# Probability transposes of an attention kernel: whole tiles by head, or 64 queries on each half of the array

## The reference, cut to what matters

```python
h = x @ w_in                                   # one projection for all head groups
# group B: 8 query heads on 2 key/value heads, dense; group A: 8 heads, masked with log multiplicities
s = q @ k.T * scale
p = softmax(s)
o = p @ v
f = concat(out_a * silu(ga), out_b * silu(gb)) @ w_out
y = layer_norm(alpha * x + f)
```

## Time and profile before

| | |
|---|---|
| median of 3 runs | 478.27 us (476.8 to 478.57) |
| profiled execution | 480.86 us, of which the span of its trace 479.0 us |
| PE busy | 438.4 us, 92% of the span |
| DVE, POOL, ACT busy | 282.1, 240.6, 217.0 us |
| probability transposes | 320 instructions |

### The profile page before, as it was taken

One profiled execution on the slowest core, in us unless ns is written; L12 is line 12 of the kernel. 1 busy time (PEld: TensorE's weight loads), 2 busy tenths in 40 slices (PEclk: granted clock), 3 DMA queues, 4 the chain that ended last, 5 costly groups with the idle time before them and its releaser, 6 DMA issues.

```text
span 479.0 us, 8874 instructions
## 1 busy us (share of the span) xinstructions
PE 438.4 (92%) x3310; PEld 403.8 (84%) x3310; DVE 282.1 (59%) x782; ACT 217.0 (45%) x499; POOL 240.6 (50%) x330
## 2 busy tenths in 40 slices
PE   1999979799889999999999999999899879999990
PEld 1999969787789999998899999999678659999990
DVE  1543675438978667464666767654576775433664
ACT  3342213443446455565555546555465774121222
POOL 1227944775644555334334854734523871455664
PEclk9999989899989999999999999999899898999996
DMA  6612212010201102001010101102000290231122
GB/s 237 252 44 62 71 30 85 22 45 23 67 8 37 46 24 65 26 22 50 28 58 22 49 23 42 45 23 67 1 23 23 73 325 1 80 96 45 68 107 90
DMA packets 23290, 29.99 MB, mean 63 GB/s; under 512 B 1872, under 2 KB 19408, under 8 KB 23248
## 3 DMA queue, kind: packets, MB, share of 16 engines
q1 hardware_dynamic: 22816, 29.30, 19.2%
q10 hardware_dynamic: 432, 0.13, 0.1%
HBM read 26.28 MB, written 3.15 MB: 61 GB/s over the span
## 4 chain that ended last, share of the span: by engine, by line
PE 67%; POOL 11%; DVE 8%; issue 6%; DMA 4%; ACT 4%; SPq 1%; ACTq 0%; DVEq 0%; POOLq 0%
PE bank L545 15%; PE bank L547 14%; PE bank L546 14%; PE bank L506 10%; PE bank L635 7%; PE bank L597 6%; DMA raw<-w_out 3%; POOL scr L1113 2%; DMA h_a<-x_prompt 2%; POOL tanh L1099 2%; POOL w_lo L1084 1%; DVE tmp_s L852 1%; ACT prob L761 1%; DVE h_qb L892 1%; DVE prob L927 1%
## 5 line engine op out<-in xcount | busy, mean ns | idle before, releaser
L545 PE MATMUL bank<-w_hi,t_lo 128*128 128x256 f32 x576 | 168.3, 292 | 2.7 <-POOL t_lo L1158 2.0
L546 PE MATMUL bank<-w_lo,t_hi 128*128 128x256 f32 x576 | 164.8, 286 | 0.0
L547 PE MATMUL bank<-w_hi,t_hi 128*128 128x256 f32 x576 | 164.7, 286 | 0.0
L1152 POOL TENSOR_SCALAR prob<-prob,den 128x512 f32<-128x512 f32 (+1 forms) x96 | 61.3, 643 | 117.0 <-DVE den L948 117.0
L545 PEld LDWEIGHTS bank<-w_hi,t_lo 128*128 128x128 f32 x576 | 112.3, 195 | 4.0 <-issue 1.4
L547 PEld LDWEIGHTS bank<-w_hi,t_hi 128*128 128x128 f32 x576 | 112.3, 195 | 0.0
L546 PEld LDWEIGHTS bank<-w_lo,t_hi 128*128 128x128 f32 x576 | 112.2, 195 | 0.0
L1084 POOL TENSOR_TENSOR w_lo<-raw,w_hi 128x512 fp32r<-128x512 f32 x52 | 67.4, 1306 | 35.2 <-ACT w_hi L714 34.6
L770 ACT ACTIVATE p_hi<-bank 128x512 fp32r<-128x512 f32 x80 | 47.2, 591 | 51.2 <-PE bank L506 51.1
L761 ACT ACTIVATE prob<-prob,nmax 128x512 f32<-128x512 f32 (+1 forms) x96 | 61.8, 645 | 15.9 <-DVE nmax L927 15.9
L714 ACT ACTIVATE w_hi<-raw 128x512 fp32r<-128x512 f32 x62 | 38.4, 629 | 48.9 <-DMA raw<-w_in 23.3
(11 more groups left out here) (110 smaller groups left out, 753.6 us busy)
## 6 DMA issues: line engine op xcount, KB each, us to landing
raw<-w_in SPq DMA_DIRECT2D x50, 256.0 KB, 2.8
raw<-w_out SPq DMA_DIRECT2D x16, 256.0 KB, 3.0
h_a<-x_prompt SPq DMA_DIRECT2D x7, 512.0 KB, 6.9
h_a<-x_sample SPq DMA_DIRECT2D x4, 512.0 KB, 9.8
y_prompt<-h_a SPq DMA_DIRECT2D x8, 256.0 KB, 2.1
y_sample<-h_a SPq DMA_DIRECT2D x4, 256.0 KB, 2.1
cst<-consts SPq DMA_DIRECT2D x1, 960.0 KB, 9.7
h_a<-x_prompt SPq DMA_DIRECT2D x2, 256.0 KB, 3.6
```

The source lines that it names most:

```text
L545: nc.tensor.matmul(out, a_lo, b_hi, start=(m == 0), stop=False)
L546: nc.tensor.matmul(out, a_hi, b_lo, start=False, stop=False)
L547: ins = nc.tensor.matmul(out, a_hi, b_hi, start=False, stop=(m == KT - 1))
L1152: ins = nc.gpsimd.tensor_scalar(e, e, den[:, s, t:t + 1], 0.5, ALU.mult, ALU.mult)
```

## The change

The four 128x128 transposes of a head become eight of 64 rows by 128 keys: queries 0 to 63 on the upper row half of the array and queries 64 to 127 on the lower, with the matching 64x64 block of the identity as the moving operand. Upper halves of both heads go to bank 4, lower halves of both to bank 5. Instructions alternate between the halves, as those of `scores` do. `pt_ready` now comes for each half, when both heads are through; `prob_high` and `prob_low` work by half (both heads) where they worked by head; the layout of `p_hi` and `p_lo` follows, and `values` of either head waits for both halves.

```diff
-        p_hi = sb("p_hi", [P, 2, 2, SEQ], F32R)
-        p_lo = sb("p_lo", [P, 2, 2, SEQ], F32R)
+        p_hi = sb("p_hi", [P, 2, 2, 2, 4, P // 2], F32R)
+        p_lo = sb("p_lo", [P, 2, 2, 2, 4, P // 2], F32R)
...
-            def prob_transposes(v):
-                pe.wait_ge(scaled, v + 1)
-                if v >= 2:
-                    pe.wait_ge(pt_lo_done, v - 1)
-                transpose_batch(pt_ps[v % 2], [prob[:, v % PRING, n * P:(n + 1) * P] for n in range(4)]) \
-                    .then_inc(pt_ready, 1)
+            def prob_transposes(w):
+                if w:
+                    pe.wait_ge(pt_lo_done, 2 * w)
+                for s in range(2):
+                    v = 2 * w + s
+                    pe.wait_ge(scaled, v + 1)
+                    for n in range(4):
+                        for half in range(2):
+                            rows = slice(P // 2 * half, P // 2 * (half + 1))
+                            at = (4 * s + n) * P // 2
+                            ins = nc.tensor.transpose(pt_ps[half][:, at:at + P // 2],
+                                                      prob[rows, v % PRING, n * P:(n + 1) * P], ident[rows, rows])
+                            if s == 1 and n == 3:
+                                ins.then_inc(pt_ready, 1)
...
-                pe.wait_ge(pt_lo_done, 2 * w + s + 1)
+                pe.wait_ge(pt_lo_done, 2 * w + 2)
...
-                o = o_ps[s][:, 0:2 * P].rearrange("p (t q) -> p t q", t=2)
+                o = o_ps[s][:, 0:2 * P].rearrange("p (t h q) -> p t h q", t=2, h=2)
...
-                        hi, lo = (a[:, s, :, n * P:(n + 1) * P] for a in (p_hi, p_lo))
+                        hi, lo = (a[:, :, :, s, n, :] for a in (p_hi, p_lo))
...
-            def prob_high(v):
-                act.wait_ge(pt_ready, v + 1)
...
+            def prob_high(w, half):
+                act.wait_ge(pt_ready, 2 * w + half + 1)
...
-                    dve.wait_ge(pt_ready, v - PRING + 1)
+                    dve.wait_ge(pt_ready, 2 * ((v - PRING) // 2) + 2)
...
-            def prob_low(v):
-                dve.wait_ge(pt_hi_done, v + 1)
...
+            def prob_low(w, half):
+                dve.wait_ge(pt_hi_done, 2 * w + half + 1)
```

More of the change, by code:

```diff
@@ L623, in values @@
                 base, keys = (QT, ST) if sample else (0, QT)
-                o = o_ps[s][:, 0:2 * P].rearrange("p (t q) -> p t q", t=2)
+                o = o_ps[s][:, 0:2 * P].rearrange("p (t h q) -> p t h q", t=2, h=2)
                 for n in range(keys):
                     if sample:
-                        hi, lo = (a[:, s, 0, :].rearrange("p (t n q) -> p t n q", n=ST, q=P)[:, :, n, :]
+                        hi, lo = (a[:, 0, :, s].rearrange("p h (t n) q -> p t n h q", n=ST)[:, :, n]
                                   for a in (p_hi, p_lo))
                     else:
-                        hi, lo = (a[:, s, :, n * P:(n + 1) * P] for a in (p_hi, p_lo))
+                        hi, lo = (a[:, :, :, s, n, :] for a in (p_hi, p_lo))
                     v = values_of(kv)[:, base + n, :]
@@ L655, in _ @@
                 if LAG <= w < NW + LAG:
-                    for s in range(2):
-                        prob_transposes(2 * (w - LAG) + s)
+                    prob_transposes(w - LAG)
                 for b in steps[w]:
@@ L763, in exps @@
                 ins.then_inc(exp_done, 1)
-            def prob_high(v):
-                act.wait_ge(pt_ready, v + 1)
[L767 to L770, removed]
+            def prob_high(w, half):
+                act.wait_ge(pt_ready, 2 * w + half + 1)
+                k = w % UNITS
+                if k % 2 == 0 and w:
+                    act.wait_ge(pv_done, group_of(2 * w - 1) + 1)
+                nc.scalar.activation(p_hi[:, k % 2, half].rearrange("p s n q -> p (s n q)"), pt_ps[half][:],
+                                     ACT.Copy).then_inc(pt_hi_done, 1)
             def copy_low(G):
@@ L809, in _ @@
                     if LAG <= w < NW + LAG:
-                        prob_high(2 * (w - LAG) + s)
+                        prob_high(w - LAG, s)
                     if w < NW:
@@ L930, in mask_max @@
                 ins.then_inc(s_masked, 1)
-            def prob_low(v):
-                dve.wait_ge(pt_hi_done, v + 1)
-                p, k, s = unit(v)
-                nc.vector.tensor_tensor(p_lo[:, s, k % 2, :], pt_ps[s][:], p_hi[:, s, k % 2, :].bitcast(F32),
-                                        ALU.subtract).then_inc(pt_lo_done, 1)
+            def prob_low(w, half):
+                dve.wait_ge(pt_hi_done, 2 * w + half + 1)
+                hi, lo = (a[:, w % UNITS % 2, half].rearrange("p s n q -> p (s n q)") for a in (p_hi, p_lo))
+                nc.vector.tensor_tensor(lo, pt_ps[half][:], hi.bitcast(F32), ALU.subtract).then_inc(pt_lo_done, 1)
             def t_low(b):
@@ L1018, in _ @@
                     if LAG <= w < NW + LAG:
-                        prob_low(2 * (w - LAG) + s)
+                        prob_low(w - LAG, s)
                     if w < NW:
```

## The result

The changed kernel takes 476.76 us (median of 20 runs, 472.14 to 480.86) beside 478.82 us of the kernel before on the same chips (20 runs): ratio 0.9944, interval 0.992 to 0.9968. It is 2.1 us faster, where 8.7 was forecast. The profiled execution took 477.14 us, its span 475.3.

A forecast was written before the change was run, and what follows sets the result against it. PE was taken to bound steps 5 to 29, chains through DVE, ACT and POOL its waits elsewhere. Gains of 10.3 us less 0.15 and 1.5 give 8.7: 478.27 - 8.7 = 469.6 us, range 465.5 to 478.

The forecast's parts named there:

- the clock: Rival: one 3.4 us half-clock stretch after PE stalls, more or less, moves time up to 1.7 us; no chance given.
- The pair, 0.06: Two half transposes, one on each row half, run side by side and take 0.06 us together.
- The stretch: Last scores to PE's next work: 0.915 us before a projection instead of 1.26, 0.805 in sample steps instead of 1.14.
- the drain and the late load: After the last half transposes: 0.10 us draining for the array-mode change, then an unhidden load, 0.11 for a projection.
- The rival of the pairs: Transpose pairs take 0.12 us, not 0.06, so the kernel gets slower, 482 us; chance 0.13.
- the one in between: Rival: transpose pairs take near 0.09 us, losing 5.9 us in 28 steps, total 476 us; chance 0.12.
- Steps 5 to 29, 9.2 - 0.15 = 9.05 us: Shorter transposes gain 9.2 us where PE is always busy; waits of values in steps 9, 14, 24 lose 0.15.
- third rival, the chains: Softmax chain or copies hold PE back, losing some 0.3 us in about 10 steps, total 473 us; chance 0.15.
- Steps 31, 32 and 35, 1.1 us: Projection work follows these transposes with no wait in the way, so 1.1 us more is gained.
- Step 37, 1.5 us: Late second head delays ACT's first copy and the values: 1.3 us lost, 2.8 with half clock, taken as 1.5.

The follow-up runs named there:

- e11: The changed kernel run once more without any edit, in another set: 474.65 us, ratio 0.9916 to the kernel before.
- e3: The changed kernel plus 60 thrown-away matmuls where PE has to wait for other engines: 469.43 us, ratio 0.9803 to the kernel before.
- e4: The kernel before plus the 60 thrown-away matmuls where PE has to wait: 477.05 us, ratio 0.9949 to the kernel before.
- e8: The changed kernel with half transposes in steps 5 to 29 alone, by head elsewhere: 471.95 us, ratio 0.987 to the kernel before.
- e9: The changed kernel with by-head transposes in steps 5 to 29, halves elsewhere: 481.04 us, ratio 1.0044 to the kernel before.
- e1: The changed kernel with by-head transposes in steps 4, 34, 37 and 39: 472.01 us, ratio 0.9843 to the kernel before.
- e7: The changed kernel issuing each head's four upper half transposes, then its four lower ones: 473.31 us, ratio 0.9914 to the kernel before.
- e6: The changed kernel with by-head transposes in step 37 alone: 475.66 us, ratio 0.991 to the kernel before.
- e2: The kernel before with the change's two later waits but its old full-height transposes: 483.75 us, ratio 1.0096 to the kernel before.

## Why the prediction was wrong, point by point

The step that failed is the rival of **the clock**: one stretch of 3.4 us more or less, up to 1.7 us either way, inside the range. In the median run it is 17 us more, and 5.5 to 6.6 us are lost by it; 19 of the 20 runs of the change have more time at 1.2 GHz than any of the 65 of the kernel before. I took the clock as noise around the forecast; it is a result of the change. That it is the clock is shown from three sides: the same program at 0.967 in place of 0.952 has a span 4 us shorter (e11), with thrown-away matmuls in both kernels the difference is 7.6 us in place of 2.1 (e3 against e4), and it is lost in the steps where PE stands and in no other (e8 against e9; in steps 5 to 29 the granted clock is 1.00 in every window shown). Ahead of each of the four falls shown PE had stood. The prediction said of these steps that gains on PE there turn into longer waits, and priced the waits at nothing. The price is that PE's work behind the wait runs at 1.2 GHz.

**The pair, 0.06** (bounds 0.055 and 0.12): 0.062, which is one matmul each 0.031. **The stretch** of 0.915 behind a projection and 0.805 in a sample step: 0.92 in step 16, and 0.71 recorded and 0.11 of a load that was not hidden, 0.82, in the sample step 29. The sum with the drain and the late load came as forecast. The rival of the pairs falls with it, and so does the one in between.

**Steps 5 to 29, 9.2 - 0.15 = 9.05 us**: 7.2 from last scores to last scores, 188.22 to 181.05, the same within 0.1 in e1, e3, e8 and e11. The seven steps with a projection give 0.33 (0.345 forecast), those with a batch of transposes and k = 2 give 0.37 or 0.38 (0.395). Most of the missing 1.9 us are in the others. The sample steps 9, 14 and 24 give 0.19 or 0.20 each, where 0.335 - 0.05 was forecast, 0.26 us less in all. Of the 0.395 of a batch step, 0.13 to 0.31 come in steps 5, 10, 15, 20 and 25, where values stand just ahead (k = 0), and 0.25 or 0.26 in the three with k = 3: 1.5 us less in these eight. The timeline of step 10 after, PE then DVE:

```profile
180.42 0.66 PE L615 MATMUL bank<-cst,prob 64*128 64x64 f32 x16
...
181.23 0.63 PE L507 MATMUL bank<-cst,h_qb 128*128 128x128 f32 x4 [0.15 <-issue]
...
180.58 0.55 DVE L969 TENSOR_TENSOR mix_t<-o_lo,mix_t 128x256 f32<-128x256 f32 x1
```

The batch writes bank 7, where the values of the second head stood, and waits until DVE has mixed them in: `mix_t` ends at 181.13 and the batch starts at 181.23. In all five steps with k = 0 it starts 0.10 us behind the end of `mix_t`, in the three with k = 3 0.14 behind. Like the forecast's third rival, the chains, it is another engine that holds PE back, but by a chain that the rival did not name, and at 1.5 us and not the 3 it was priced at. PE's waits in steps 5 to 29 grew from 0.00 to 181.05 - 180.44 = 0.61 us.

**Steps 31, 32 and 35, 1.1 us**: steps 32 and 35 give 0.37 and 0.33; step 31 can't be separated from the clock in the two profiles, but takes 7.39 us in e4 and 7.06 in e3, 0.33 less.

**Step 37, 1.5 us** (1.3 to 2.8): The mechanism is as described. PE, ACT and DVE in step 37 after, the place of the earlier trace rows:

```profile
374.29 0.46 PE L615 MATMUL bank<-cst,prob 64*128 64x64 f32 x8 [0.59 <-POOL prob L1163]
375.14 0.69 PE L615 MATMUL bank<-cst,prob 64*128 64x64 f32 x8 [0.39 <-POOL prob L1163]
...
375.86 0.60 ACT L780 ACTIVATE p_hi<-bank 128x512 fp32r<-128x512 f32 x1 [1.76 <-PE bank L615]
...
377.68 0.69 DVE L947 TENSOR_TENSOR p_lo<-bank,p_hi 128x512 fp32r<-128x512 f32 x1 [0.33 <-ACT p_hi L780]
...
378.52 0.55 PE L646 MATMUL bank<-p_hi,v_st 128*128 128x256 f32 x1 [2.69 <-DVE p_lo L947]
```

ACT waits for both heads, the second `p_lo` ends at 378.37 and the values start at 378.52, 2.69 us after PE fell idle and 5.79 behind the first scores of step 37, where it was 380.76 - 377.14 = 3.62 before. From step 37's last scores to the next step's it takes 9.39 us, 2.83 more than before. That is the upper bound of the forecast, and its reason came true as well: these values run at 1.2 GHz. But the next two steps take back 1.42 and 0.34, so the bound was right for the place and too high for the kernel. For steps 30 to 39 together 1.1 - 1.5 = -0.4 was forecast, and with the added matmuls in both kernels (e4, e3) it is -0.6: what was given back beyond that is the clock's.

**What stays open.** Which stretch falls to 1.2 GHz differs between executions of one program, and a stand is not always followed by a fall. In e11 PE stood for 2.5 us in step 30, and the clock stayed up:

```profile
329.40:332.80 3.40, 0.93 (x6) 1.00 0.00 0
332.80:336.20 3.40, 3.40 (x33) 1.00 0.01 2
```

Undoing the halves in four steps (e1) and issuing them half by half (e7) left the clock at 0.969 and 0.967, undoing them in step 37 alone (e6) at 0.956. No run tells why the ones raised it and the other didn't. The longer waits without the shorter work (e2) did not lower it; the shorter work without the longer waits was not run, so whether it takes both stays open.

## What to carry to other kernels

In this kernel the gain on PE held where PE never stands: about 7.2 us in steps 5 to 29, whatever the rest did. Where PE stands, look at the granted clock before pricing a change at nothing: here the change there put more of the work behind the stands at 1.2 GHz. When a change to PE moves the time less than its busy time, compare several runs by their time at 1.2 GHz before looking for a wait. Thrown-away matmuls in the stands both test this and, here, keep the gain.

## What the hardware did that I had not expected

**The order of issue does not bind the two row halves.** In e7, sixteen half transposes take 0.72 us although four uppers are issued ahead of four lowers. If starts followed the order of issue, the four lowers could only begin with the fourth upper, and so on, and sixteen would take about 0.97 (12 periods of 0.062 and 0.223). The Trainium skill, "TensorE: Matmul & The Clock Gate" (Part 3, "The mechanism"), states that matmuls start and end in program order, without reordering; for matmuls on separate row halves this trace does not agree, with its 0.72 against 0.97.

**Added work makes the kernel faster.** 60 matmuls that nobody reads make the kernel before 0.5% faster (0.9949 [0.9933, 0.9965]) and the changed one, by the medians, 476.76 - 469.43 = 7.3 us faster.
